# Four feed-forward layers by Strassen products: another order in the first column block, x sums for pairs of tiles, a last down product in pairs of tiles

## The reference

```
h = rms_norm(x, norm)
return (jax.nn.silu(h @ w_gate) * (h @ w_up)) @ w_down
```

## Time and profile before

| | |
|---|---|
| time, median of 3 runs | 3410.07 us (3406.92 to 3413.01) |
| the profiled execution | 3404.96 us, its span 3403.1 us |
| TensorE (PE) busy | 94% of the span |
| VectorE (DVE) busy | 64% |
| ScalarE (ACT) busy | 44% |
| DMA engines, mean | 28.6% for the queue of the weights |
| mean granted TensorE clock | 0.969 of full speed |

### The profile page before, as it was taken

How to read it: one execution, slowest core, us unless ns; L and a number is a source line. 1 busy time by engine, 2 the same in 40 slices (tenths; PEclk the granted TensorE clock), 3 DMA queues, 4 the chain that set the end, 5 groups by cost and what they waited for, 6 DMA issues and landing times.

```text
span 3403.1 us, 39021 instructions
## 1 busy us (share of the span) xinstructions
PE 3193.8 (94%) x15002; PEld 2591.2 (76%) x15002; DVE 2189.3 (64%) x3436; ACT 1488.2 (44%) x2291; POOL 76.2 (2%) x153
## 2 busy tenths in 40 slices
PE   9999999999979995999999899969999998969998
PEld 7888776778768894888877677858889676748887
DVE  7333788644576766765678765367566677777656
ACT  5222556533353433533456544235334464344333
POOL 0000001000000000000010000000000100000000
PEclk9999999999989997999999899989999999979999
DMA  4333332223323322332242222323332544223231
GB/s 150 99 93 92 105 93 80 81 81 99 111 75 99 93 72 81 108 96 87 78 115 81 62 87 78 96 87 99 96 97 64 103 66 78 62 81 106 87 93 62
DMA packets 244554, 304.09 MB, mean 89 GB/s; under 512 B 11665, under 2 KB 198417, under 8 KB 244369
## 3 DMA queue, kind: packets, MB, share of 16 engines
q1 hardware_dynamic: 237616, 284.73, 28.6%
q0 software_dynamic: 6608, 16.79, 1.8%
q10 hardware_dynamic: 144, 0.10, 0.0%
HBM read 293.17 MB, written 2.10 MB: 87 GB/s over the span
## 4 chain that ended last, share of the span: by engine, by line
PE 82%; DVE 11%; ACT 5%; issue 1%; DMA 1%; DVEq 0%; ACTq 0%; SPq 0%
PE bank L221 80%; DVE k_sc L183 2%; PE bank L227 2%; DVE k_wl L173 2%; ACT k_sc L217 1%; ACT k_wh L217 1%; DVE k_x L183 1%; DVE k_acc L173 1%; DVE k_sc L173 1%; DVE k_xraw L173 1%; ACT L211 0%; DVE k_sc L178 0%; DVE k_sc L199 0%; DVE k_uf L183 0%; ACT k_uf L217 0%
## 5 line engine op out<-in xcount | busy, mean ns | idle before, releaser
L173 DVE TENSOR_TENSOR k_wl<-k_raw,k_wh 128x1024 fp32r<-128x1024 f32 (+2 forms) x373 | 435.8, 1172 | 525.7 <-ACT k_wh L217 497.4
L217 ACT ACTIVATE k_wh<-k_raw 128x1024 fp32r<-128x1024 f32 (+2 forms) x373 | 376.1, 1013 | 535.9 <-PE bank L221 377.2
L221 PE MATMUL bank<-k_xh,k_wh 128*128 128x512 f32 x1224 | 506.3, 414 | 7.4 <-ACT k_wh L217 4.9
L221 PE MATMUL bank<-k_xl,k_wh 128*128 128x512 f32 x1224 | 479.2, 391 | 1.6 <-DVE k_xl L173 1.6
L221 PE MATMUL bank<-k_xh,k_wl 128*128 128x512 f32 x1224 | 479.5, 392 | 0.3
L221 PE MATMUL bank<-k_wh,k_s 128*128 128x512 f32 (+1 forms) x1120 | 337.9, 383 | 116.3 <-ACT k_sc L217 116.3
L173 DVE TENSOR_TENSOR k_wl<-k_xraw,k_wh 128x1024 fp32r<-128x1024 f32 (+1 forms) x234 | 269.9, 1154 | 223.7 <-ACT k_wh L217 213.9
L217 ACT ACTIVATE k_wh<-k_xraw 128x1024 fp32r<-128x1024 f32 (+1 forms) x234 | 234.6, 1003 | 345.5 <-PE bank L221 264.9
L221 PEld LDWEIGHTS bank<-k_wh,k_s 128*128 128x128 f32 x1120 | 209.8, 192 | 149.3 <-ACT k_sc L217 118.2
L221 PEld LDWEIGHTS bank<-k_xh,k_wh 128*128 128x128 f32 x1224 | 231.3, 189 | 73.2 <-issue 18.1
L221 PE MATMUL bank<-k_gn,k_wh 128*128 128x512 f32 x864 | 272.9, 397 | 1.4 <-ACT k_wh L217 1.4
(11 more groups left out here) (368 smaller groups left out, 5828.2 us busy)
## 6 DMA issues: line engine op xcount, KB each, us to landing
k_raw<-in_w_in SPq DMA_DIRECT2D x153, 512.0 KB, 3.7
k_xraw<-in_ffn_w_down SPq DMA_DIRECT2D x48, 512.0 KB, 3.5
k_xraw<-in_ffn_w_up SPq DMA_DIRECT2D x42, 512.0 KB, 4.7
...
```

What stands on the lines that cost most here:

```text
L173: return q.op(lambda e: e.tensor_tensor(out, a, b, op), cost(out))
L217: return self.A.op(lambda e: e.activation(out, a, f, bias=bias, scale=scale), c)
L221: fn = lambda e: e.matmul(out, l, r, start=start, stop=stop, skip_group_check=True)
```

## The change

It has four parts.

1. In the first column block of a stage the products come in the order P1, P2, P6, P5, P7 in place of P6, P2, P7, P5 after P1. The weight combination T3 is made after P6 there.
2. `whole_x` in a stage of `STRASSEN` only issues the high part of `k_uf`. After every second tile it hands both tiles to a generator, `pair_sums`, which takes the place of `scaled_blocks` and `other_sums`. It writes each kind of instruction for both tiles in turns (`set_pairs` for the parts): for tiles 0 to 3 the low part of `k_uf`, S3 and the squares, for tiles 4 to 7 the low part, S2, the squares, S1 and S4.
3. The last `down` takes two tiles at a time: the first three pairs with the first half of the hidden tiles, then with the second, then the fourth pair with both. It drains each pair as soon as it is done, so that only tiles 6 and 7 come at its end.
4. `w_out` reads the parts of the merged tiles from two arrays of its own (`k_m0mhi`, `k_m0mlo`), so that the fourth split pair is open before `w_out` and `w_out_2`, and stays open from one Strassen stage to the next and through the last one.

The number of matmuls is the same (11119 rows on TensorE with the branch, in both).

```diff
+        if gname in STRASSEN:
+            c = VEC[gname][0] + k
+            h = self.UF[k][0]
+            w = [tok, self.t_vec] + list(free)
+            self.late.append((k, w, self.ac(w, h, self.X[k][:, 0:width(h)], ACT.Identity, scale=self.vec[:, c:c + 1])))
+            if k % 2:
+                self.bg.append(self.pair_sums(self.late, gname))
+                self.late = []
+            return
         s, fs = self.take(self.SC)
-        if gname in STRASSEN:
-            self.scaled_blocks(k, [tok, self.t_vec] + list(free), gname)
...
+    def pair_sums(self, pair, gname):
 
         c = VEC[gname][0]
         g = lambda i: self.vec[:, c + i:c + i + 1]
...
+        X = self.X
+        lo_, hi_ = slice(0, 256), slice(256, 512)
+        for k, w, th in pair:
+            h, lo = self.UF[k]
+            self.uf[k] = (th, self.stt(w + [th], lo, X[k][:, 0:width(h)], g(k), h.bitcast(F32), ALU.mult, ALU.subtract))
+        sc = []
+        for k, w, _ in pair:
+            s, fs = yield from self.wait_slot(self.SC)
+            sc.append((s, self.ts(w + fs, s[:, lo_], X[k][:, hi_], g(k), None, ALU.mult)))
+        k0 = pair[0][0]
+        sets = lambda name, toks, part: self.set_pairs(name, k0 % 4, [s[:, part] for s, _ in sc], toks, pair[0][1] + pair[1][1])
+        if k0 < 4:
+            t = [self.stt([t], s[:, hi_], X[k][:, lo_], g(k), s[:, lo_], ALU.mult, ALU.subtract) for (s, t), (k, _, _) in zip(sc, pair)]
+            t = sets("S3", t, hi_)
+        else:
+            t1 = [self.stt([t], s[:, lo_], X[k - 4][:, hi_], g(k - 4), s[:, lo_], ALU.mult, ALU.add) for (s, t), (k, _, _) in zip(sc, pair)]
+            t2 = [self.stt([t], s[:, hi_], X[k - 4][:, lo_], g(k - 4), s[:, lo_], ALU.mult, ALU.subtract)
+                  for (s, _), (k, _, _), t in zip(sc, pair, t1)]
+            t = sets("S2", t2, hi_)
+        sq = []
+        for k, w, _ in pair:
+            s, fs = yield from self.wait_slot(self.SC)
+            sq.append((s, self.ac(w + fs, s, X[k], ACT.Square)))
+        for (s, ta), (k, _, _) in zip(sq, pair):
+            self.square(k, s, ta)
+        if k0 >= 4:
+            yield
+            sets("S1", t1, lo_)
+            yield
+            t = [self.stt([t], s[:, hi_], X[k][:, lo_], g(k), s[:, hi_], ALU.mult, ALU.add) for (s, _), (k, _, _), t in zip(sc, pair, t)]
+            t = sets("S4", t, hi_)
+        for (s, _), t in zip(sc, t):
+            self.SC.put(s, [t])
...
+    def set_pairs(self, name, j0, srcs, toks, free):
+        dst = [self.SX[name][j0 + i] for i in range(2)]
+        hs = [self.ac([t] + free, d[0], a, ACT.Copy) for d, a, t in zip(dst, srcs, toks)]
+        los = [self.tt([h] + free, d[1], a, d[0].bitcast(F32), ALU.subtract) for d, a, h in zip(dst, srcs, hs)]
+        for i in range(2):
+            self.sx[(name, j0 + i)] = (hs[i], los[i])
+        return los
...
+        keep = nextg is None or nextg in STRASSEN
         lent = [self.MB.free.pop() for _ in range(2)]
         self.LIN.free += lent
-        self.open_pair(start)
         self.bg.append(self.norm_tok())
-        self.bg.append(self.other_sums(gname, start))
...
+                t3 = ((q("T3", "B22", "B12") + (ALU.subtract,) + q("B12")),)
                 one = {
                     "P1": ((ld("B11", h), ld("B12", h)), (), "B11", ((q("T1", "B12", "B11") + (ALU.subtract,) + q("B11")),), ()),
-                    "P6": ((ld("B22", h), (key("T2", h), None)), ((q("T2", "T1", "B22") + (ALU.subtract, None)),), "T2", (), ()),
-                    "P2": ((ld("B21", h),), (), "B21", ((q("T3", "B22", "B12") + (ALU.subtract,) + q("B12")),), ()),
+                    "P6": ((ld("B22", h), (key("T2", h), None)), ((q("T2", "T1", "B22") + (ALU.subtract, None)),), "T2",
+                           () if b else t3, ()),
+                    "P2": ((ld("B21", h),), (), "B21", t3 if b else (), ()),
...
+            if last:
+                steps = [(kb, m) for kb in range(2) for m in (0, 2, 4)] + [(0, 6), (1, 6)]
+            else:
+                steps = [(kb, q + m) for q in (0, 4) for kb in range(2) for m in (0, 2)]
+            bk = {}
+            for kb, mp in steps:
+                i, wh, wl, th, tl = self.chunk(wd, l, r0 + kb * nf * P, nf, mp * P, 256, not last or keep)
...
+                if kb:
+                    for m in range(mp, mp + 2):
+                        self.bg.append(ddown(m, bk[m][0], done[m - mp]))
+                    self.quantum(1)
...
-        run(0, "P1")
         for b in range(nb):
-            run(b, "P6")
-            run(b, "P2")
-            if b and b % 2 == 0:
-                down(b // 2 - 1, False)
-            run(b, "P7")
-            run(b, "P5")
+            if b == 0:
+                for name in ("P1", "P2", "P6", "P5", "P7"):
+                    run(b, name)
+            else:
+                run(b, "P6")
+                run(b, "P2")
+                if b % 2 == 0:
+                    down(b // 2 - 1, False)
+                run(b, "P7")
+                run(b, "P5")
             if b + 1 < nb:
                 run(b + 1, "P1")
             run(b, "P4")
             run(b, "P3")
-        self.close_pair()
+        if not keep:
+            self.close_pair()
+        self.uf, self.sx = [None] * 8, {}
         down(nb // 2 - 1, True)
         self.flush()
-        if nextg not in STRASSEN:
+        if not keep:
             self.close_units()
-        self.sx = {k: v for k, v in self.sx.items() if nextg in STRASSEN and k[0] == "S2"}
-        if nextg not in STRASSEN:
-            self.uf = [None] * 8
...
-        pe = self.PE.last()
-        mt = [self.split_to([mtok[k], pe], tl(MRG, k), self.XH[k], self.XL[k]) for k in range(8)]
-        self.open_units(self.marks())
-        self.linear("w_out", l, 0, 8, 0, D, lambda k: (self.XH[k], self.XL[k], mt[k][0], mt[k][1]),
-                    self.add_x(nextg, self.marks(), 0.5))
+        free = self.marks()
+        self.open_units(free)
+        self.open_pair(free)
+        mt = [self.split_to([mtok[k], free[0]], tl(MRG, k), tl(MHI, k), tl(MLO, k)) for k in range(8)]
+        self.linear("w_out", l, 0, 8, 0, D, lambda k: (tl(MHI, k), tl(MLO, k), mt[k][0], mt[k][1]),
+                    self.add_x(nextg, free, 0.5))
...
@@ -1931,6 +1951,7 @@
         self.flush()
         self.open_units(self.marks())
+        self.open_pair(self.marks())
         self.linear("w_out_2", 0, 512, 4, 0, D, lambda k: (tl(Y, yi(k)), tl(Y, yi(k) + 1), yt[4 + k][0], yt[4 + k][1]),
                     self.add_x(nextg, self.marks()))
         self.flush()
```

More of the change, by code:

```diff
@@ L694, in other_sums @@
-    def other_sums(self, gname, free):
-        c = VEC[gname][0]
-        g = lambda i: self.vec[:, c + i:c + i + 1]
-        for j in range(4):
-            q, fq = yield from self.wait_slot(self.SC)
-            ta = self.ts(fq, q[:, 0:256], self.X[j][:, 256:512], g(j), None, ALU.mult)
-            tb = self.stt([ta], q[:, 256:512], self.X[j][:, 0:256], g(j), q[:, 0:256], ALU.mult, ALU.subtract)
-            self.sx[("S3", j)] = self.pair_of([tb] + free, q[:, 256:512], self.SX["S3"][j])
-            self.SC.put(q, [self.sx[("S3", j)][1]])
+        X = self.X
@@ L2015, in build @@
         self.UF = [(UF[:, uo(k):uo(k) + uw(k)], UF[:, 3072 + uo(k):3072 + uo(k) + uw(k)]) for k in range(8)]
-        self.uf, self.sx, self.sj = [None] * 8, {}, [None] * 4
+        self.uf, self.sx, self.late = [None] * 8, {}, []
         self.nsq, self.acc_free, self.acc_tok, self.r_free = 0, [], None, []
```

68 lines of the change are left out of this document (18 added, 50 removed).

## The result

The changed kernel takes 3349.65 us (median of 4 runs, 3348.50 to 3350.12), against 3409.58 us (3406.92 to 3413.01) before: a ratio of 0.9823, with a 95% interval of 0.9806 to 0.9840. That is 59.9 us less. The profiled executions stand 54.8 us apart: 3404.96 before, 3350.12 now, with a span of 3348.3.

The account below looks back on a forecast made before the run. TensorE, 94% busy, was taken as the bound, with only its idle time to win, mostly at four Strassen starts. 12.0 + 12.0 + 7.8 + 7.7 + 7.5 + 2.0 = 49.0 us; 3404.96 became 3356, given as median 3361; range 3337 to 3392.

Parts of the forecast that it names:

- The bound: Strassen starts: P6 waits for the copy of P1's banks behind VectorE's sums and splits, starting at u + 9.4.
- u: The end of S4 of tiles 6 and 7 on VectorE, forecast at 941.9 for n2_0.
- The pair: VectorE, tiles 4 to 7: two tiles in turns take 10.5 us, tile by tile 13.9.
- pairs gain nothing: Rival, VectorE: idle time turns into other waits, a pair costs 13.9 us, 32.8 given back, 3394; chance 0.12.
- The clock: Behind each start's gap: P6, P5, P7 run at the low level for 8.1 us again, losing 4.05 us.
- the clock is back at once: Rival, four starts: the shorter gap brings no low level, 4.05 us more saved each, 16.2, 3345; chance 0.20.
- The other starts: Starts of n1_1 and nf2, VectorE bound from the first pair or drain on: 7.8 and 7.7 us won.
- The mixers: Earlier drains in the last down win 7.5 us at the third mixer, 2.0 at the second.
- The wait of 5.86 at the third mixer: Sign: TensorE's idle time there for the last split falls from 5.86 us to below 3.
- stay low until P7's end: Rival, four starts: P6, P5, P7 at half rate, 12.75 us more per start, 51 in all, 3412; chance 0.04.
- case of late splits: Rival, Strassen stages: products wait for their splits, 0.2 us per half product costing 67 us, 3429; chance 0.04.
- Costs at nothing: Priced at zero: merged parts' new home, T3 behind P6, fourth pair open earlier, table load, DMA, nf2's last down.

Follow-up runs that it names:

- experiment 1: The changed kernel with each x tile's sums written in one piece, tile after tile, not two tiles in turns: 3374.88 us.
- Experiment 5: The changed kernel with 28 more matmuls, their sums unread, between the halves of P2 in each Strassen stage's first block: 3351.33 us.
- experiment 2: The changed kernel with the old product order P1, P6, P2, P7, P5 in the first block and T3 made at P2: 3384.09 us.
- Experiment 3: The changed kernel with the last down taking four tiles at a time again where a mixer follows (n1_1 and n2_1): 3350.41 us.
- Experiment 10: The changed kernel with every last down taking four tiles at a time, in the old order: 3343.86 us.
- experiment 6: The changed kernel with the fourth split pair opened at each Strassen stage's start and closed ahead of its last down: 3351.73 us.

## Why the prediction was right, and where it was not

The forecast was 3361, the range 3337 to 3392; 3349.65 lies in it. Part of that is luck: the starts gave 21.7 us more than forecast, and the mixers 7.5 and the rests 3.6 less. Step by step:

- **The bound.** Right: VectorE's sums, the splits behind them and the copy of P1's banks set the start. P6 came 9.3 us behind u at n2_0 (forecast 9.4). That u came at 941.93 (forecast 941.9) is in part chance: the stage's P1 stood at 926.63 and not at 924.49, pair 6, 7 began 0.6 us late and took 0.6 less.
- **The pair.** 10.5 us per pair was close to 9.95. The rival "pairs gain nothing" falls with experiment 1. Undoing the turns costs 25 us. The Trainium skill's rule on chained instructions (page "VectorE: DVE Perf Modes", section "The DRAIN you can't avoid") is not contradicted, since the gain is VectorE's idle time for ScalarE, 0.48 us twice per tile, which that rule does not speak of.
- **The clock: the step that failed.** The prediction had P6, P5 and P7 lose "4.05" us at each start, "with the clock at its low level for 8.1 us again". TensorE did work at that level, for 7.3 us of n2_0 (942.47 to 949.74), but it was P2's second half that lay in it, and P6 had to wait for its copy until 951.22 anyway. Experiment 5 took the low level away and gained nothing; experiment 2 put P6 into it and lost 3.7 to 6.4 us a start. Four times 4.05 is 16.2 of the 21.7 us by which the starts beat the forecast. From P6 to block 1 it took 16.6 us at every start, and not 20.85. The rival "the clock is back at once" had the number for these starts, but by another mechanism than it named: the level did fall, on another piece. The sign that the prediction gave, a clock of 0.50 for some 8 us behind P6's start, did not come.
- **The other starts.** n1_1 and nf2 gave 13.2 and 13.7 for 7.8 and 7.7. Less the clock, 1.4 and 2.0 us are left (1.2 and 1.1 at n2_0 and n2_1), the size of the error of the walk from their first drains (u at n1_1 26.6 us behind P1, forecast 28.55).
- **The mixers: mis-sized, in part of the wrong sign.** The third mixer's last drain was to stand 1.1 us behind the end of `down`; a double split of 2.36 us and the whole chain of tile 6, 2.8, stand ahead of it, and it came at 2607.10, 5.1 behind 2601.96. The start won 3.7, the stage 2.4, in place of 7.5. The second mixer lost 4.4 in place of winning 2.0: with the new order of drains three rotary steps stand on VectorE ahead of a step that empties two banks, where one stood before. TensorE waited 3.38 us for `k_m1qkva` at 1718.76, and the granted clock in the stretch from 1708 to 1728 was 0.83, where it had been 1.00 (the rows of the changed kernel, then the same place before):

```profile
1718.76 0.79 PE L221 MATMUL bank<-k_wh,k_xh 128*128 128x512 f32 x1 [3.38 <-DVE k_m1qkva L173]
```

```profile
1708.00:1728.00 20.00, 16.62 (x62) 13.09 (x61) 19.19 (x27) 2.43 (x3) 8.42 (x17) 0.83 0.53 142
```

```profile
1740.00:1760.00 20.00, 20.00 (x85) 15.61 (x84) 14.00 (x19) 10.05 (x14) 6.47 (x13) 1.00 0.38 100
```

Experiment 3 took the wait away and gave 3.4 of the 4.4 us back. The wait of 5.86 at the third mixer, which was to fall below 3, fell to 4.86.

- **The other rivals.** The clock did not stay low until P7's end: it is 1.00 from 950 on. The Trainium skill's advice to run matmuls back to back (page "Perfetto Trace Analysis", section "Matmul Optimizations") has its price here, the low level behind the gap, but on a piece that had the time. The splits were not late as a rule: of the 29.6 us of waits for `k_wh`, 23.4 are the four gaps ahead of P2's second half (6.68, 4.77, 6.67, 5.30). The case of late splits was priced at 3429; 3361 and 67 are 3428.
- **Part 3 of the change** was forecast to win 9.5 us at the mixers and a share at n1_1. Experiment 10 shows that without it the kernel is 5.8 us faster. "VectorE is bound from the first pair on" was true of the queue, but not of the engine: waits for ScalarE's splits stood between the drains.
- **The parts together.** Undoing part 1 costs 34.4 us, the turns of part 2 25.2, and undoing part 3 wins 5.8; if they may be added, they make 53.8 of the 59.9. What the rest of part 2 is worth, S1, S3 and S4 written with each pair and not behind all tiles, was not run by itself, and neither was the new home of the merged tiles.
- **Costs at nothing.** The fourth pair (experiment 6) is confirmed. The rests of the stages were not quite free: 3.6 us, 1.1 at each of the first three, with a new wait of 0.81 us for `k_gn` ahead of the first `down` of a stage. "It is wrong if the blocks behind the first take longer than before" was a sign of the prediction's own, and it did come, by that 1.1.

The profiled executions moved by 54.8 us, the medians by 59.9; the profiled execution of before lay 4.6 below its median, and that of the changed kernel does not. The forecast kept that distance on both sides.
